# A step of a hybrid transformer on one core: two weight chunks with places of their own at the head, and a triangular inverse spread over four quarters of the matmul array

## The chip, the cores and the metric

The kernel runs as one program on one core of a Trainium2 chip. The metric is the device time of one execution in microseconds (us); lower is better. A core has five engines, each with its own queue of instructions: TensorE (PE, matmuls into PSUM), VectorE (DVE), ScalarE (ACT), GpSimd (POOL) and SyncE (SP), which here only issues DMA transfers. They wait for each other by semaphores.

## The reference

One inference step of a small backbone: two layers, width 1024, 128 context tokens and 512 latent tokens, all in float32. For each layer:

```python
h = modulate(rmsnorm(x, p['norm_mix_g']), mod[0], mod[1])       # mod = silu(c) @ w_ada + b_ada
q, k, v, u_r, u_f = split_projection(h, p['w_in'])              # 1024 -> 2176 columns
o_attn = latent_attention(axial_rope(q), axial_rope(k), v, k_ctx, v_ctx, p['attn_sink'])
o_rwkv, _, _ = rwkv_mix(u_r, s_ctx[:, 0], s_ctx[:, 1], p)       # both directions, 4 heads of 64
o_fnet = fourier_mix(u_f)
x = x + g1 * (concat(o_attn, o_rwkv, o_fnet) @ p['w_out'])      # then norm, SwiGLU (2816), residual

def step(S, inp):                                               # the scan inside rwkv_mix
    r_t, w_t, k_t, v_t, kk_t, a_t = inp
    S = (S * w_t[:, :, None, :]
         - jnp.einsum('bhvk,bhk->bhv', S, kk_t)[..., None] * (kk_t * a_t)[:, :, None, :]
         + v_t[..., None] * k_t[:, :, None, :])
    return S, jnp.einsum('bhvk,bhk->bhv', S, r_t)
```

Outputs are both token streams after a last norm, the context's keys and values, and the final scan states.

## The kernel before, in words

Channels lie on the 128 partitions and all 640 tokens on the free axis, so x is eight tiles of 128x640. A float32 weight is split on the chip: ACT copies it into a high half of the type float32r (`weight_high`), POOL subtracts to get the low half (`weight_low`), and three matmuls make one product.

**Weights and the ring.** SP loads the weights in chunks of mostly 1 MB, in the fixed order of the list CHUNKS, into a ring of four slots (`ring`). A chunk is issued only when the chunk four places earlier has been used (`ada_done` for modulation weights "ada", `wl_ready` for projection weights "rw"). For layer 0 the order begins ada 0 to 3, rw 0, ada 4 to 7, rw 1. Two ada chunks make one call of `ada_rows` (L957), 32 thin matmuls written into a PSUM bank; a copy (`row_copy`, DVE or ACT) and `ada_cols` (L966) turn them into columns of the table `mod`.

**The head of layer 0.** PE transposes x in ten halves of 128x512 (L863); ACT copies each out of PSUM. ACT squares x tile by tile into the two buffers `sq`, PE adds them over channels (`norm_part`, L872), ACT takes the root, DVE the reciprocal, PE spreads it (`inverse(0)`). Then PE does `ada_rows(0)`, `inverse(0)`, `ada_cols(0)`, some idle matmuls for warming (`warm`), `ada_rows(1)` and `ada_cols(1)`. DVE builds the first half of `mod` and the gain, scales x, ACT adds the shift, DVE makes the low half, and PE starts the first two units of the projection with `ada_rows(2)` and `ada_rows(3)` between their halves. POOL issues 15 small parameter loads first, then its memsets (`mn_zero`), for which ACT waits before its first copy.

**The recurrence.** The scan over tokens is done in chunks of 64 tokens. A pair is a 128x128 block: two chunks (`ck`) by two heads (`hd`). Four pairs make a group, and the five groups of a layer run in two calls: groups 0 and 1, then, after the rest of the attention, groups 2 to 4. Each pair p owns PSUM banks 2p and 2p+1. For a group:

1. `token_tiles`: four transposes a pair (L1273 to L1276), which ACT copies to SBUF (L1755).
2. Products of the scaled rows (L1306, L1309, L1312): twelve 64x64 or 64x128 matmuls a pair; each float32 matmul counts as two instructions.
3. DVE multiplies the product A B by the mask of the first level (L2235), the other products by the masks (L2237), and adds the unit matrix (L2242): T0.
4. The inverse of the unit triangular matrix of 64x64, by six levels of doubling. PE first puts T0 and its transpose into PSUM (L1322, L1325). Levels 1 to 5: PE multiplies B by the inverse so far (L1334), DVE masks the product (P1, L2256), PE adds P1 Y and X P1 to what stands in PSUM (L1341, L1346; in the last level L1349 makes another product), and ACT copies both, 256 columns (XY, L1767). Every step goes over the four pairs in turn; a pair's step is at `ps` rows of its own chunk, so inputs and output lie on the same half of the partitions.
5. Two more products (L1356; L1364 to L1373), then the chain over chunks, one after the other: L1392 makes the next state, L1397 the output, DVE scales and adds (L2287, L2300, L2303). In the chain of groups 0 and 3, at steps 4 and 5, PE issues two pairs' token tiles of the next group ahead.

POOL takes no part in the recurrence but for loads of states (L804), stores of final states (L825) after group 2, and half the scaling (`by_r_and_rate`, L814). The next weights after it are those of w_out (NPROJ).

Of the kernel before, what the change touches and what calls it, by code (L numbers as in the profile page):

```python
# [12 lines left out]
KT = D // 128  # L13
# [14 lines left out]
SLOTS = 4  # L28
# [38 lines left out]
CHUNKS = chunk_order()  # L67
# [206 lines left out]
def build(nc, I, O):  # L274
# [7 lines left out]
    with ctx:  # L282
# [180 lines left out]
        w_ready = [sem(f"w_ready{s}") for s in range(SLOTS)]  # L463
        wh_ready = sig("wh_ready", NUNIT)
# [47 lines left out]
        prod_ps, l0_sb, lp_sb, t0_sb = (sig(x_, n2) for x_ in ("prod_ps", "l0_sb", "lp_sb", "t0_sb"))  # L512
# [25 lines left out]
        xT_ps, xT_sb, c_ready = sem("xT_ps"), sem("xT_sb"), sem("c_ready")  # L538
# [28 lines left out]
        def unit_weights(l, u):  # L567

            _, ck, g, nk = UNITS[u]
            n = CHUNK_AT[(l,) + ck]  # L570
            raw_w = ring[:, n % SLOTS, 0:2 * nk * 128].rearrange("p (k c) -> p k c", k=nk)
# [16 lines left out]
            return n, raw_w[:, :, 128 * g:128 * g + 128], parts[0], parts[1]  # L588
# [60 lines left out]
        def _(e):  # L649
# [25 lines left out]

            for n, (l, kind, i) in enumerate(CHUNKS):
                if (kind, i) == ("rw", 2):
                    tables_of(l)
# [64 lines left out]
        def _(e):  # L743
            own = Own(e, pool_own)
            params(e, 0)

# [5 lines left out]
            nc.gpsimd.memset(csil[:, :, :], 0.0).then_inc(mn_zero, 1)  # L752
            e.wait_ge(mn_zero, 5)
            e.wait_ge(xT_ps, 11)
            for l in range(DEPTH):

                def weight_low(u):
                    n, raw_w, hi, lo = unit_weights(l, u)
                    e.wait_ge(wh_ready.sem, wh_ready.upto(l, u + 1))
                    nc.gpsimd.tensor_tensor(lo, raw_w, hi, SUB).then_inc(wl_ready(), 1)  # L760
# [87 lines left out]
        def _(e):  # L848
# [7 lines left out]
            for t in range(5):  # L856
                e.wait_ge(ld_x[t], 16)
                for g in range(2):
                    n = 2 * t + g
                    if n >= 2:  # L860
                        e.wait_ge(xT_sb, n - 1)
# [5 lines left out]
            e.wait_ge(xT_sb, 10)  # L867
# [15 lines left out]
            for l in range(DEPTH):  # L883
# [5 lines left out]
                def chunk(name, of=None):  # L889
                    n = CHUNK_AT[(l if of is None else of,) + name]  # L890
                    e.wait_ge(w_ready[n % SLOTS], READY[n])
                    return ring[:, n % SLOTS, :]
# [6 lines left out]
                def norm_part(la, which, k):  # L899

                    e.wait_ge(sq_ready.sem, sq_ready.upto(la, which * KT + k + 1))
# [136 lines left out]

                if l == 0:
                    for k in range(KT):  # L1040
                        norm_part(0, 0, k)

                e.wait_ge(ld_prow[l], 16 * 15)
                lat, cx = begin(("small", 0))
                tr(lat[:, 0:NPR], prow[:, :], ident[0:NPR, 0:NPR]).then_inc(acc_ready(), 1)
                if l == 0:
                    ada_rows(0, l)
                    inverse(0)
                    ada_cols(0, l)
                    warm(8)  # L1050
                    ada_rows(1, l)
                    ada_cols(1, l)
# [204 lines left out]
                def recurrence(first, last_group, items_before, pairs_before):  # L1257
# [4 lines left out]

                    def token_tiles(g, n):
# [14 lines left out]
                    tiled = 0  # L1278
                    for g in range(first, last_group):
# [6 lines left out]
                        if g > first and tiled < ng:  # L1286
# [10 lines left out]
                        for n in range(tiled, ng):  # L1297
                            token_tiles(g, n)
                        tiled = 0
                        for n, (p, ht, d, t) in enumerate(group):  # L1300
                            e.wait_ge(tok_sb.sem, tok_sb.upto(l, base + n + 1))
                            H, A_, R_, K_, B_ = row_of[ht]
                            tiles = [(hd, rows_of[hd], ck, rows_of[ck], slice(128 * t + 64 * ck, 128 * t + 64 * ck + 64))
                                     for ck in range(2) for hd in range(2)]
                            for hd, hs, ck, cs, c in tiles:
# [1289 lines left out]
```

## Time and profile before

| what | value |
|---|---|
| three runs | 1905.29, 1906.85 (median), 1908.67 us |
| the profiled execution | 1905.69 us, of which the span from the first to the last instruction is 1903.9 us |
| mean granted clock of TensorE | 0.994 of full speed |
| DMA | 161.25 MB, mean 85 GB/s over the span |

The profile is that of one execution. A busy engine is one with an instruction running; PE's weight loads (PEld) run beside its matmuls. An arrow in brackets names what ended the idle time before a row. Rows with the same line, one after the other, stand merged with their count.

### The profile page before, as it was taken

What the parts mean: (1) busy time and instruction counts of PE and PEld (TensorE: products, weight loads), DVE (VectorE), ACT (ScalarE), POOL (GpSimd) and SP (SyncE); (2) the same over time, 40 slices, a digit from 0 to 9 for tenths busy, and PEclk for the clock granted to TensorE, in tenths of its full rate; (3) what the DMA queues carried; (4) which work ended last, traced back from release to release, by engine and by line L of the source; (5) the groups of instructions that cost most, each with busy time, mean ns of one, the idle gap of its engine ahead of it and who ended that gap; (6) DMA issues with size and microseconds to landing.
All of it is one profiled execution on the core that took longest, in us unless ns stands there. A gap on an engine that the chain in (4) does not pass through costs nothing. (4 is left out here: it accounts for less than half of the span.)

```text
span 1903.9 us, 48376 instructions
## 1 busy us (share of the span) xinstructions
PE 1806.2 (95%) x20973; PEld 1704.9 (90%) x20973; DVE 1053.7 (55%) x2344; ACT 828.6 (44%) x1736; POOL 348.7 (18%) x230
## 2 busy tenths in 40 slices
PE   6899889999999999999999997989999999999997
PEld 5899678888989999999989986969888999999997
DVE  2433866655196483747453358474536828556563
ACT  4332655553165253434433256455424525434352
POOL 3233300011211203020233440000032030111112
PEclk8999999999999999999999999999999999999999
DMA  8753600001632423232327343000012132321311
GB/s 266 249 152 103 180 4 3 3 7 27 199 89 68 111 67 99 63 94 73 94 80 214 101 137 84 4 2 7 26 45 65 53 105 62 95 81 62 96 63 56
DMA packets 215950, 161.25 MB, mean 85 GB/s; under 512 B 21969, under 2 KB 213147, under 8 KB 215739
## 3 DMA queue, kind: packets, MB, share of 16 engines
q1 hardware_dynamic: 213818, 156.13, 27.9%
q8 instruction: 167, 2.74, 0.6%
q0 software_dynamic: 1920, 2.03, 0.3%
q14 instruction: 45, 0.36, 0.1%
HBM read 154.99 MB, written 3.15 MB: 83 GB/s over the span
## 5 line engine op out<-in xcount | busy, mean ns | idle before, releaser
L2365 DVE SCALAR_TENSOR_TENSOR x<-PS,mod,x 128x320 f32<-128x320 f32 (+2 forms) x240 | 90.7, 433 | 295.1 <-PE PS L998 295.1
L1033 PE MATMUL PS<-T_hi,wsplit 128*128 128x320 f32 x768 | 170.0, 309 | 0.0
L997 PE MATMUL PS<-in_hi,win 128*128 128x320 f32 x480 | 150.6, 321 | 1.6 <-ACT mix L1621 0.9
L760 POOL TENSOR_TENSOR SfR<-ring,SfR 128x768 fp32r<-128x768 f32 (+1 forms) x24 | 41.1, 1711 | 582.0 <-ACT SfR L1571 582.0
L998 PE MATMUL PS<-in_hi,win 128*128 128x320 f32 x480 | 144.9, 309 | 0.0
L1767 ACT ACTIVATE mix<-PS 128x256 f32<-128x256 f32 x240 | 92.5, 385 | 98.5 <-PE PS L1346 43.0
L997 PE MATMUL PS<-hid_hi,wsplit 128*128 128x320 f32 x440 | 133.1, 310 | 0.0
L998 PE MATMUL PS<-hid_hi,wsplit 128*128 128x320 f32 x440 | 132.5, 309 | 0.0
L1033 PEld LDWEIGHTS PS<-T_hi,wsplit 128*128 128x128 f32 x768 | 128.5, 188 | 0.0
L1033 PE MATMUL PS<-h_hi,wsplit 128*128 128x320 f32 x576 | 127.6, 309 | 0.0
L1033 PE MATMUL PS<-T_lo,wsplit 128*128 128x320 f32 x384 | 118.7, 309 | 0.0
L1852 ACT ACTIVATE wsplit<-Sf 128x512 fp32r<-128x512 f32 x96 | 59.8, 629 | 130.0 <-DVE Sf L2415 72.3
L2435 DVE TENSOR_TENSOR E<-E,PS 128x320 f32<-128x320 f32 x120 | 58.5, 488 | 87.5 <-PE PS L1033 87.2
L760 POOL TENSOR_TENSOR win<-ring,win 128x1024 fp32r<-128x1024 f32 x30 | 72.5, 2417 | 175.5 <-ACT win L1571 175.3
L1571 ACT ACTIVATE win<-ring 128x1024 fp32r<-128x1024 f32 x30 | 31.8, 1061 | 159.1 <-PE PS L998 136.2
L760 POOL TENSOR_TENSOR wsplit<-ring,wsplit 128x768 fp32r<-128x768 f32 (+2 forms) x42 | 74.5, 1779 | 119.5 <-ACT wsplit L1571 119.5
L1033 PEld LDWEIGHTS PS<-h_hi,wsplit 128*128 128x128 f32 x576 | 96.4, 188 | 0.0
L997 PEld LDWEIGHTS PS<-in_hi,win 128*128 128x128 f32 x480 | 90.2, 188 | 6.1 <-issue 4.7
L998 PEld LDWEIGHTS PS<-in_hi,win 128*128 128x128 f32 x480 | 90.3, 188 | 2.4 <-issue 2.4
L2256 DVE TENSOR_TENSOR mix<-PS,lvl 128x128 f32<-128x128 f32 x200 | 49.2, 291 | 75.2 <-PE PS L1334 75.0
L1033 PE MATMUL PS<-h_lo,wsplit 128*128 128x320 f32 x288 | 89.0, 309 | 0.0
L997 PEld LDWEIGHTS PS<-hid_hi,wsplit 128*128 128x128 f32 x440 | 82.6, 188 | 0.5 <-issue 0.5
(492 smaller groups left out, 5543.2 us busy)
## 6 DMA issues: line engine op xcount, KB each, us to landing
ring<-in_w_ada SPq DMA_DIRECT2D x48, 1024.0 KB, 7.4
ring<-in_ffn_w_in SPq DMA_DIRECT2D x88, 512.0 KB, 5.0
ring<-in_ffn_w_out SPq DMA_DIRECT2D x16, 768.0 KB, 4.3
ring<-in_ffn_w_out SPq DMA_DIRECT2D x16, 640.0 KB, 4.0
ring<-in_w_in SPq DMA_DIRECT2D x8, 1024.0 KB, 6.7
ring<-in_w_in SPq DMA_DIRECT2D x10, 512.0 KB, 5.8
ring<-in_w_in SPq DMA_DIRECT2D x16, 256.0 KB, 5.7
ring<-in_w_out SPq DMA_DIRECT2D x16, 256.0 KB, 6.5
```

Of the source, the lines that this page charges most:

```text
L760: nc.gpsimd.tensor_tensor(lo, raw_w, hi, SUB).then_inc(wl_ready(), 1)
L997: mm(lat[:, 0:TH], w, v[:, 0:TH], start=(n == 0), stop=(n == total - 1))
L998: last = mm(cx[:, 0:TH], w, v[:, TH:T], start=(n == 0), stop=(n == total - 1))
L1033: last = mm(bank[:, 0:TH], (w_lo if p == 1 else w_hi)[:, k, :], (v_lo if p == 2 else v_hi)[:, k, :], start=(q in (A11, A12, S1_) and k == ...
L1571: act(hi, raw_w, ACT.Copy).then_inc(wh_ready(), 1)
L1767: act(XY[p].rearrange("p a t -> p (a t)"), ps[2 * p + 1][:, 0:256], ACT.Copy).then_inc(xy_sb(), 1)
L1852: act(hi, raw_b, ACT.Copy).then_inc(bh_ready(), 1)
L2256: V.tensor_tensor(P1[p], ps[2 * p][:, 0:128].rearrange("p (a t) -> p a t", a=2), lvl[:, d, lv:lv + 1, :].to_broadcast([128, 2, 64]), MUL). ...
L2365: last = V.scalar_tensor_tensor(x[:, m, a:b], bank[:, at:at + b - a], mod[:, gate_at + m, s:s + 1], x[:, m, a:b], MUL, ADD)
L2435: V.tensor_tensor(v, v, bank[:, 0:TH], op).then_inc(ps_taken(), 1)
```

## The change

Two chunks, rw 0 and ada 4 of layer 0, leave the ring's order and get places in a buffer that is free at that time; SP issues them after the first four ring chunks, with no wait. On PE `ada_rows(0)` goes ahead of the norm sums; `ada_cols(0)` and `ada_rows(1)` go ahead of `inverse(0)`, and the warming matmuls behind `ada_cols(1)`; the parameter transpose stands amid the sums. Copies of x out of PSUM and squares of x are taken by ACT and DVE in turn; the copy of c and of the parameters goes to DVE; POOL's memsets go ahead of its loads.

In the recurrence A B is formed transposed, into the other half of the partitions, together with the other products; POOL adds the unit matrix to it in place; DVE's masks contain the unit matrix too, so that P1 is the unit matrix plus the masked product and PSUM need not accumulate. X moves to the other bank and the other half of the partitions, so that the matmuls for X and Y of one level lie on different quarters of the array and are issued in turn. The fifth level's extra product goes into its first part. In the chains of groups 0 and 3, at steps 6 and 7, the products of two pairs of the next group are issued ahead.

The lists and the loads, on SP:

```diff
-CHUNKS = chunk_order()
+SIDE = ((0, "rw", 0), (0, "ada", 4))
+CHUNKS = [c for c in chunk_order() if c not in SIDE]
...
+        side_at = [mixv(S2_AT, SLOT_W), mixv(22150, SLOT_W)]
...
             for n, (l, kind, i) in enumerate(CHUNKS):
+                if n == SLOTS:
+                    side(0)
+                    side(1)
```

On POOL; the last call stands after the stores of the final states:

```diff
+                def unit_diagonals(g):
+
+                    for n, (p, ht, d, t) in enumerate(GROUPS[g]):
+                        e.wait_ge(lp_sb.sem, lp_sb.upto(l, 4 * g + n + 1))
+                        nc.gpsimd.tensor_tensor(LP[p][:, :, BA, :], LP[p][:, :, BA, :],
+                                                eye64[:, :].unsqueeze(1).to_broadcast([128, 2, 64]), ADD).then_inc(
+                                                    diag_sb(), 1)
+
                 state_in(0)
                 by_r_and_rate(0)
+                unit_diagonals(0)
                 state_in(1)
+                for g in range(1, 4):
+                    unit_diagonals(g)
...
+                unit_diagonals(4)
```

On PE, the head:

```diff
                 if l == 0:
+                    ada_rows(0, l)
+                    e.wait_ge(xT_sb[0], 5)
+                    e.wait_ge(xT_sb[1], 5)
                     for k in range(KT):
                         norm_part(0, 0, k)
-
-                e.wait_ge(ld_prow[l], 16 * 15)
-                lat, cx = begin(("small", 0))
-                tr(lat[:, 0:NPR], prow[:, :], ident[0:NPR, 0:NPR]).then_inc(acc_ready(), 1)
-                if l == 0:
-                    ada_rows(0, l)
+                        if k == 3:
+                            small()
+                    ada_cols(0, l)
+                    ada_rows(1, l)
                     inverse(0)
-                    ada_cols(0, l)
+                    ada_cols(1, l)
                     warm(8)
-                    ada_rows(1, l)
-                    ada_cols(1, l)
```

On PE, the recurrence:

```diff
+                    halves = [(hd, ck, rows_of[ck], rows_of[1 - ck]) for hd in range(2) for ck in range(2)]
+                    def products(g, n):
...
+                        for hd, hs, cs, os, c in tiles:
+                            mm(ps[2 * p + hd][os, 128:192], H[hs, B_ + d, c], H[hs, A_ + d, c], start=True, stop=True)
+                        for hd, hs, cs, os, c in tiles:
+                            mm(ps[2 * p + hd][cs, 0:128], H[hs, K_ + d, c], H[hs, d:d + 3:2, c], start=True, stop=True)
+                        for hd, hs, cs, os, c in tiles:
+                            last = mm(ps[2 * p + hd][cs, 192:256], H[hs, B_ + d, c], H[hs, R_ + d, c],
+                                      start=True, stop=True)
...
-                        for n in range(tiled, ng):
+                        for n in range(ahead_, ng):
                             token_tiles(g, n)
...
+                        for n in range(ahead_, 2):
+                            products(g, n)
+                        ahead_ = 0
+                        products(g, 2)
+                        first_inverse(g, 0)
+                        products(g, 3)
+                        for n in range(1, ng):
+                            first_inverse(g, n)
...
-                                for hd, ck, cs in halves:
-                                    last = mm(ps[2 * p][cs, 64 * hd:64 * hd + 64], LP[p][cs, hd, BA, :],
-                                              XY[p][cs, 2 + hd, :], start=True, stop=True)
+                                for hd, ck, cs, os in halves:
+                                    if lv == 5:
+                                        mm(ps[2 * p][cs, 128 + 64 * hd:192 + 64 * hd], LP[p][cs, hd, KA, :],
+                                           TOK[p][cs, tV, 64 * hd:64 * hd + 64], start=True, stop=True)
+                                    last = mm(ps[2 * p + 1][cs, 128 + 64 * hd:192 + 64 * hd], LP[p][os, hd, BA, :],
+                                              XY[p][os, 2 + hd, :], start=True, stop=True)
...
-                                for hd, ck, cs in halves:
-                                    mm(b1[cs, 64 * hd:64 * hd + 64], P1[p][cs, hd, :], XY[p][cs, hd, :],
-                                       start=False, stop=(lv == 5), skip_group_check=True)
...
+                                for hd, ck, cs, os in halves:
                                     if lv < 5:
-                                        last = mm(b1[cs, at_x], XY[p][cs, hd, :], P1[p][cs, hd, :],
-                                                  start=False, stop=(lv == 4), skip_group_check=True)
...
+                                        mm(ps[2 * p + 1][os, 64 * hd:64 * hd + 64], XY[p][cs, hd, :], P1[p][cs, hd, :],
+                                           start=True, stop=True)
+                                    last = mm(ps[2 * p][cs, 64 * hd:64 * hd + 64], P1[p][cs, hd, :], XY[p][cs, hd, :],
+                                              start=True, stop=True)
...
+                            if g in (0, 3) and i in (6, 7):
+                                products(g + 1, i - 6)
+                                ahead_ = 2
```

On ACT:

```diff
+                        def inverse_copy(lv, n):
...
+                            src = ps[2 * p][:, 0:256] if lv == 5 else PS[:, 2 * p:2 * p + 2, 0:128]
```

On DVE:

```diff
-                            V.tensor_tensor(P1[p], PS[:, 2 * p:2 * p + 2, 256:320],
-                                            lvl[:, d, 0:1, :].to_broadcast([128, 2, 64]), MUL).then_inc(l0_sb(), 1)
...
-                            V.tensor_tensor(T0[p], P1[p], eye64[:, :].unsqueeze(1).to_broadcast([128, 2, 64]),
-                                            ADD).then_inc(t0_sb(), 1)
+                        def first_level(n):
+                            p, ht, d, t = group[n]
+                            e.wait_ge(diag_sb.sem, diag_sb.upto(l, base + n + 1))
+                            V.tensor_tensor(T0[p], LP[p][:, :, BA, :], lvl[:, d, 0:1, :].to_broadcast([128, 2, 64]),
+                                            MUL).then_inc(t0_sb(), 1)
+
+                        factors(0)
+                        for n in range(1, ng):
+                            factors(n)
+                            first_level(n - 1)
+                        first_level(ng - 1)
```

And in the table of the levels' masks:

```diff
+        lv[:, :, n] += (i == t)[:, None, :]
```

## Rows read from the trace of the kernel before

**Rows 1.** The page's first and second part: busy time; granted clock by slice.

```profile
PE 1806.2 (95%) x20973; PEld 1704.9 (90%) x20973; DVE 1053.7 (55%) x2344; ACT 828.6 (44%) x1736; POOL 348.7 (18%) x230
PEclk8999999999999999999999999999999999999999
```

**Rows 2.** Busy time by stretch: stretch, length, each engine, then PEclk, DMA share, GB/s.

```profile
255.60:317.50 61.90, 57.19 (x1818) 54.51 (x1818) 34.93 (x119) 26.50 (x67) 2.48 (x4) 1.00 0.02 5
15.00:20.00 5.00, 3.30 (x20) 2.42 (x18) 0.00 (x0) 4.02 (x8) 0.00 (x0) 1.00 1.10 348
25.00:30.00 5.00, 5.00 (x81) 3.49 (x81) 1.15 (x1) 2.56 (x5) 0.00 (x0) 0.50 0.00 0
69.60:255.60 186.00, 175.52 (x1589) 158.18 (x1589) 97.64 (x161) 83.02 (x189) 61.97 (x33) 1.00 0.48 140
```

**Rows 3.** Timeline, two levels of the first group: start, length, then engine and line.

```profile
264.22 0.89 DVE L2256 TENSOR_TENSOR mix<-PS,lvl 128x128 f32<-128x128 f32 x4
264.56 0.45 PE L1341 MATMUL PS<-mix 64*64 64x64 f32 x8
266.48 1.10 PE L1334 MATMUL PS<-mix 64*64 64x64 f32 x32
267.41 0.40 PE L1341 MATMUL PS<-mix 64*64 64x64 f32 x8
268.09 1.79 ACT L1767 ACTIVATE mix<-PS 128x256 f32<-128x256 f32 x4 [1.01 <-PE PS L1346]
269.28 1.10 PE L1334 MATMUL PS<-mix 64*64 64x64 f32 x32
```

**Rows 4.** Timeline of PE, products of the second group.

```profile
290.04 0.29 PE L1306 MATMUL PS<-h 64*64 64x64 f32 x8
290.15 0.40 PE L1309 MATMUL PS<-h 64*64 64x128 f32 x8
```

**Rows 5.** ACT copies: timeline of four of 512 columns, then groups by form.

```profile
256.58 2.07 ACT L1755 ACTIVATE mix<-PS 128x512 f32<-128x512 f32 x4
...
L1755 ACT ACTIVATE mix<-PS 128x512 f32<-128x512 f32 x40 | 21.5, 599 | 27.2 <-PE PS L1276 27.0
L1767 ACT ACTIVATE mix<-PS 128x256 f32<-128x256 f32 x240 | 92.5, 385 | 98.5 <-PE PS L1346 43.0 <-PE PS L1325 33.4 <-PE PS L1349 10.2
```

**Rows 6.** Timeline between products and levels, second group; then DVE by form.

```profile
289.44 0.34 PE L1306 MATMUL PS<-h 64*64 64x64 f32 x8
292.49 0.68 DVE L2237 TENSOR_TENSOR mix<-PS,masks 128x512 f32<-128x512 f32 x1
293.49 0.68 DVE L2237 TENSOR_TENSOR mix<-PS,masks 128x512 f32<-128x512 f32 x1
295.00 1.13 PE L1334 MATMUL PS<-mix 64*64 64x64 f32 x32
...
L2242 DVE TENSOR_TENSOR mix<-mix,eye 128x128 f32<-128x128 f32 x40 | 11.3, 281 | 0.0
```

**Rows 7.** POOL additions by form; then timeline of POOL beside DVE.

```profile
L830 POOL TENSOR_TENSOR mix<-mix 128x640 f32<-128x640 f32 x12 | 18.9, 1574 | 16.9 <-ACT mix L1520 16.9
L760 POOL TENSOR_TENSOR wsplit<-ring,wsplit 128x768 fp32r<-128x768 f32 x20 | 36.9, 1854 | 59.0 <-ACT wsplit L1571 59.0
...
69.59 2.69 POOL L760 TENSOR_TENSOR win<-ring,win 128x1024 fp32r<-128x1024 f32 x1
69.94 2.49 DVE L2045 SCALAR_TENSOR_TENSOR mix<-mix,par 128x128 f32<-128x128 f32 x1
```

**Rows 8.** Timeline of PE at the head.

```profile
24.94 1.39 PE L872 MATMUL PS<-mix,mats 128*32 128x160 f32 x16 [0.23 <-ACT mix L1520]
26.64 3.64 PE L957 MATMUL PS<-ring,csil 128*32 128x128 f32 x64
35.42 1.96 PE L957 MATMUL PS<-ring,csil 128*32 128x128 f32 x64
52.33 1.95 PE L957 MATMUL PS<-ring,csil 128*32 128x128 f32 x64 [2.95 <-DMA ring<-in_w_ada]
```

More of the change, by code:

```diff
@@ L463, in build, with chunk_at, landed @@
         w_ready = [sem(f"w_ready{s}") for s in range(SLOTS)]
+        side_ready = [sem(f"side_ready{s}") for s in range(len(SIDE))]
+        side_at = [mixv(S2_AT, SLOT_W), mixv(22150, SLOT_W)]
+        def chunk_at(key):
+            return side_at[SIDE.index(key)] if key in SIDE else ring[:, CHUNK_AT[key] % SLOTS, :]
+        def landed(e, key):
+            if key in SIDE:
+                e.wait_ge(side_ready[SIDE.index(key)], 16)
+            else:
+                e.wait_ge(w_ready[CHUNK_AT[key] % SLOTS], READY[CHUNK_AT[key]])
         wh_ready = sig("wh_ready", NUNIT)
@@ L1538, in norm_shift @@
                     last.then_inc(h_ready(), 1)
-            e.wait_ge(xT_sb, 10)
+            for q_ in range(2):
+                e.wait_ge(xT_sb[q_], 5)
             for l in range(DEPTH):
@@ L1549, in _ @@
                 if l == 0:
-                    for k in range(KT):
-                        norm_square(0, 0, k)
+                    for k in range(0, KT, 2):
+                        if k >= 2:
+                            e.wait_ge(sq_used.sem, sq_used.upto(0, k - 1))
+                        act(sq[:, 0, :], x[:, k, :], ACT.Square).then_inc(sq_first[0], 1)
                 norm_root(l, 0)
-                free, lat, cx = ready(("small", 0))
-                act(par[:, :], lat[:, 0:NPR], ACT.Copy).then_inc(free(), 1)
-                taken(e, l, ("small", 0))
-                act(omka[:, :], par[:, PR_KA:PR_KA + 2], ACT.Copy, scale=-1.0, bias=1.0).then_inc(par_ready(), 1)
+                if l > 0:
+                    free, lat, cx = ready(("small", 0))
+                    act(par[:, :], lat[:, 0:NPR], ACT.Copy).then_inc(free(), 1)
+                    taken(e, l, ("small", 0))
+                    act(omka[:, :], par[:, PR_KA:PR_KA + 2], ACT.Copy, scale=-1.0, bias=1.0).then_inc(par_ready(), 1)
                 def weight_high(u, of=None):
@@ L1764, in recurrence @@
                         for lv in range(6):
-                            for n, (p, ht, d, t) in enumerate(group):
-                                e.wait_ge(xy_ps.sem, xy_ps.upto(l, 6 * base + lv * ng + n + 1))
-                                act(XY[p].rearrange("p a t -> p (a t)"), ps[2 * p + 1][:, 0:256],
-                                    ACT.Copy).then_inc(xy_sb(), 1)
+                            for n in range(ng):
+                                inverse_copy(lv, n)
                         for n, (p, ht, d, t) in enumerate(group):
@@ L2019, in _ @@
                 if l == 0:
+                    row_copy(0)
+                    free, lat, cx = ready(("small", 0))
+                    V.tensor_copy(par[:, :], lat[:, 0:NPR]).then_inc(free(), 1)
+                    taken(e, l, ("small", 0))
+                    V.tensor_scalar(omka[:, :], par[:, PR_KA:PR_KA + 2], -1.0, 1.0, MUL, ADD).then_inc(par_ready(), 1)
                     norm_inverse(l, 0)
-                    row_copy(0)
                     row_copy(1)
```

151 lines of the change are left out of this document (81 added, 70 removed).

## The prediction

> **What bounds the kernel now.** I read four views: the page, the busy time by stretch, the timeline of the engines, and the groups by line and form. The page's first part shows TensorE (PE) busy for 95% of the span, VectorE (DVE) for 55%, ScalarE (ACT) for 44%; its second part shows a granted clock below nine tenths in the first slice alone [rows 1]. So most of the time is PE's, and only what shortens PE's own work, or a wait of PE, is worth anything.
>
> By stretch, two places are different from the dense matmuls. The recurrence runs in four stretches, two per layer, ten groups in all; in the first of them PE is busy for 57.2 of 61.9 us, with the clock at 1.00 [rows 2], and the others look the same. These are small 64x64 matmuls, so the question is how fast PE takes them. And at the head, from 25 to 30 us, the DMA engines move nothing (0 GB/s, after 348 GB/s from 15 to 20 us), while PE works at half clock, 0.50, which is 1.2 instead of 2.4 GHz [rows 2]: the ring's four slots are full of modulation weights that nobody has used yet.
>
> **The levels of the inverse.** In the timeline one level of a group of four pairs is: 32 matmul instructions at L1334, then 64 at L1341 and L1346, then the next level. It begins at 266.48 us and the next at 269.28: 2.80 us, of which the first part takes 267.41 - 266.48 = 0.93 and the second 269.28 - 267.41 = 1.87 [rows 3]. That is 29 ns for each instruction in both, and PE has no gap: a level is PE's. All these matmuls lie on two of the four 64x64 quarters of the array (rows 0-63 to columns 0-63, rows 64-127 to columns 64-127).
>
> The change gives the second part four quarters: X goes to the crossed quarters and Y to the straight ones, taken in turn. The first part moves to the crossed quarters, but there are still only two, so it stays at 0.93. What a matmul on four quarters costs is in the trace already: the products of L1306 use all four, and eight instructions of 64 columns take 290.15 - 290.04 = 0.11 us, 14 ns each [rows 4]. So the second part falls to 64 x 14.5 ns = 0.93, and PE's work in a level from 2.80 to 1.86. In the fifth level the matmul that was last in the second part goes to the first, onto free quarters, at nothing; the saving is the same.
>
> The Trainium skill speaks against this: its page "TensorE: Matmul & The Clock Gate", section "Wait — 56ns, not 53.3ns?", says that the start of one matmul follows the start of the one before by 25 ns at least, however narrow they are. By that the second part would take 64 x 25 ns = 1.6 us and a level about 2.6 (an estimate from that page); the 14 ns above do not agree with it.
>
> Is PE then still what bounds a level? PE takes instructions in order, so the second part of pair 0 stands behind the first part of pair 3, which waits for ACT's copy of pair 3 of the level before. The loop: from the start of the second part to ACT's first copy now 268.09 - 267.41 = 0.68, of which 0.47 is PE's own time for that pair [rows 3]; with 0.23 it is 0.45 to 0.50, I take 0.50. Then three more copies: ACT's mean for this copy is 385 ns and its neighbours overlap; four copies of 512 columns at 599 ns take 2.07 us, a spacing of 0.49, 0.11 less than their duration [rows 5]. So 256 columns are spaced by about 0.275: 0.83 for three. The last copy takes 0.385 and I allow 0.10 to reach PE (from DVE's first product at 264.22, some 0.28 long by its like in rows 6, to PE at 264.56 it is 0.06 [rows 3]). Then the first part of pair 3, 0.23. Sum 0.50 + 0.83 + 0.485 + 0.23 = 2.05 us. DVE is not in it: its product of pair 0 has long ended. Low end: PE alone, 1.86. High end: copies that don't overlap, 0.45 apart, 2.57. I take 2.05, because the overlap is in the rows. Saved: 0.75 a level, 5 levels x 10 groups = 50 levels: **37.5 us** (11 to 47).
>
> **Before the levels.** From the first product to the first level a group takes 295.00 - 289.44 = 5.56 us; DVE sets it with three operations a pair, and the pairs follow each other by 1.00 us (292.49 to 293.49) [rows 6]; two of the three are of 128x128, the third of 128x512. The change drops one of the small ones, about 0.2 of the 1.00 as it overlaps its neighbour, and puts an addition on GpSimd (POOL) between the two others, so the pairs come at 0.8 but each has POOL in its chain. No row shows an addition of 128x128 on POOL: 640 columns take 1.57 us and 768 take 1.85, so 128 by that slope about 0.45; ends 0.28 (DVE's own time for such a one [rows 6]) and 1.57. I take 0.5 plus 0.2 to start; it lies beside the next pair's DVE work, and shows once, behind the last pair. In POOL's queue ahead of it are only loads of states and work for the first head pair that is finished before the group begins; behind it stand the stores of the states and the low halves of w_out, needed after the recurrence. DVE has an operation of another task between this stage and the first level in every group, so that the earlier end is partly given back there. I count 0.2 us for a group whose products all still come after the token tiles (6 groups). In the other 4 groups two pairs' products are issued in the chain of the group before, where PE waits for DVE; that brings them, and DVE's first factors, forward by about 1 us. PE's next chain step behind such a product comes 0.44 later. Together **5 us**, with ends of 0 and 12 by POOL's ends.
>
> POOL and DVE can also block each other. At 69.94 us a DVE operation of 128x128 with two SBUF inputs took 2.49 us beside a POOL operation that ran from 69.59 for 2.69 [rows 7], where a product of that size and kind of inputs takes 0.28 [rows 6]: it waited till POOL was done. The Trainium skill, "SBUF — State Buffer", section "Who interferes with whom", has the rule: a DVE operation with two SBUF inputs and a POOL operation that reads SBUF exclude each other, and the first to start holds the port. In this case the T0 product has two SBUF inputs and meets POOL's addition for the next pair; but it starts first, as its engine needs no wake-up, and the factors beside it read PSUM. If POOL is first each time, it is 0.4 us for each pair, 1.6 per group, 16 us in all. I take it at 0.
>
> **The head.** Now: the norm's sums, a pair of them 1.39 us, paced by squares on ACT alone; then the first row products at 26.64, 3.64 us at half clock; only then is a slot free, and the fourth row products start at 52.33, after a wait of 2.95 us for their weights [rows 8]. After: the two side chunks follow the four ring chunks without a wait; at 348 GB/s [rows 2] a chunk of 1 MB takes 3.0 us. The four are in by 24, so the side chunks by 30 and ada chunks 5 to 7 by 39, if their slots come free in time; they do, if the first and second rows end before about 33. The first rows need two chunks (about 18 us); at half clock they end near 21.8. Then four pairs of norm sums at about 1.7 (the squares of a pair now run together, but each waits for its buffer): 28.5. The second rows at half clock, 3.6: 32. From their end to the point where PE is ready for the fourth rows it is now 52.33 - 2.95 - (35.42 + 1.96) = 12.0 us [rows 8], work that the change leaves as it is: 44. The weights come at 39.5, or 42.8 if POOL's mask tables, 1.2 MB, are carried in between. So 44 for 52.33, and I call it **8.5 us** with the copies of x. At full clock PE would be there at 39 and the weights decide: at most 13; with the norm sums late by two more pairs, 5. From 69.6 to 255.6 us PE is busy for 175.5 of 186 [rows 2] and the view of waits names no DMA there, so the gain is kept. Moving the copies of x, the parameter columns and POOL's memsets costs nothing that is late: the first rows wait for weights until 18 us.
>
> **Sum.** 37.5 + 5 + 8.5 = 51 us, off the profiled execution's 1905.7 (its span is 1903.9): 1854.7. That execution is 1.2 us under the median of the three runs. Forecast: 1855.
>
> **Rivals.**
> 1. ACT bounds the levels: copies from two banks don't overlap, 2.57 us a level. For it: ACT already needs 0.385 a copy and PE leaves less room. Against: the 0.49 spacing [rows 5]. Saves 11.5 + 13.5: 1881.
> 2. The four quarters don't overlap in this order, since X and Y of a pair come from the same rows back to back, while the products of L1306 alternate rows. Then a level stays at 2.80 and 13.5 is left: 1892. Against: the 14 ns [rows 4]. By the floor of the Trainium skill's page "TensorE: Matmul & The Clock Gate", named above, a level of 2.6 would give 1882, an estimate that no row bears out.
> 3. POOL's addition costs 1.57, near the row for 640 columns, and holds DVE: the stage before the levels takes some 2.5 us longer in each group, 25 less 5 and the rest as forecast: 1885.
> 4. Slower: the granted clock falls in the levels. PE will have gaps of about 0.2 us in each level where it had none, and at the head the clock fell to 0.50 after a stretch with PE busy 3.30 of 5 us [rows 2]. A level at half clock is 2 x 1.86 plus some 0.2 of latency, 3.9 us instead of 2.05; the gain of 51 is gone when 28 of 50 levels run so. With all: 1905.7 + 50 x 1.1 - 8.5 = 1952. Against: PE would still be busy for nine tenths of a level, and in the recurrence, whose chains make it wait as it is, the clock stands at 1.00 [rows 2].
>
> **How the numbers follow.** Forecast or near it 0.72; rival 1 0.10; rival 2 0.07; rival 3 0.05; rival 4 or another loss of that size 0.06. The forecast's own range, from the ends above taken two thirds of the way, is 1838 to 1872; with all low ends at once it is 1834. To leave out no more than 0.2 it reaches to rivals 1 to 3: 1836 to 1892. No change means within 0.2%, 3.8 us, about what a measurement of this kernel can tell: only a mix of rivals ends there. Faster 0.91, same 0.03, slower 0.06.
>
> **What would show it.** In the timeline the second part of a level with 16 instructions a pair in 0.23 us (rival 2: 0.47), the levels 2.05 apart, and PE's waits at the first part released by ACT; ACT's four copies 0.28 apart (rival 1: 0.45). POOL's additions near 0.5 us and DVE's T0 at 0.28, without long ones. At the head no stretch without DMA before 39 us, the second rows done by 32, the fourth begun near 44. The clock at 1.00 in the four stretches. The forecast is wrong if the levels don't come closer than 2.5 us.

## The result, and the profile after

The changed kernel takes 1893.27 us, the median of five runs (1883.86 to 1896.24); the kernel before took 1906.85 beside it. The ratio is 0.992, with a 95% interval of 0.9896 to 0.9944: about 14 us faster where 51 were forecast. The profiled execution took 1893.27 us, its span is 1891.5.

First the page of the changed kernel: busy time, granted clock by slice, and the queue that carries instructions (packets, MB, share).

```profile
PE 1766.6 (93%) x20973; PEld 1661.0 (88%) x20973; DVE 1063.6 (56%) x2316; ACT 805.5 (43%) x1723; POOL 364.1 (19%) x270
PEclk9999999999999999999999999999999999999999
...
q8 instruction: 166, 2.72, 0.6%
```

PE is busy for 40 us less than in [rows 1], with the same number of matmuls, but the span is only 12 us shorter: work went, waits came. Busy time by stretch of the changed kernel (the columns are those of [rows 2]): the first recurrence stretch, the head from 25 us, the levels of the first group, and its chain.

```profile
248.19:309.05 60.86, 50.34 (x1818) 46.61 (x1816) 34.42 (x110) 23.21 (x66) 5.31 (x12) 0.93 0.02 5
...
25.00:30.00 5.00, 4.53 (x98) 3.42 (x99) 2.82 (x6) 4.18 (x5) 0.58 (x1) 1.00 1.10 349
255.26:268.37 13.11, 10.54 (x494) 10.11 (x488) 6.62 (x22) 5.85 (x20) 1.42 (x3) 1.00 0.03 9
...
274.00:282.00 8.00, 7.03 (x113) 5.86 (x116) 3.41 (x15) 1.19 (x2) 0.00 (x0) 0.64 0.01 2
```

The stretch of [rows 2] was 61.9 us with PE busy for 57.2; it is 60.9 with PE busy for 50.3. The clock is 1.00 in the levels, but 0.64 in the chain behind them. From 25 to 30 us DMA moves 349 GB/s where it moved nothing. The head did what was forecast (PE's timeline, second and fourth row products):

```profile
27.07 1.95 PE L994 MATMUL PS<-ring,csil 128*32 128x128 f32 x64
...
43.38 1.84 PE L994 MATMUL PS<-ring,csil 128*32 128x128 f32 x60 [0.90 <-DMA ring<-in_w_ada]
```

The fourth begin 8.95 us sooner than in [rows 8], and the recurrence 7.7 us sooner (248.19 for 255.89, first token tile). What is missing is in the recurrence. ACT's copies in the levels of the first group, one row per level unless a level is broken up:

```profile
257.29 1.21 ACT L1815 ACTIVATE mix<-PS 128x256 f32<-128x256 f32 x4 [1.34 <-PE PS L1398]
259.32 1.21 ACT L1815 ACTIVATE mix<-PS 128x256 f32<-128x256 f32 x4 [0.82 <-PE PS L1398]
261.36 0.94 ACT L1815 ACTIVATE mix<-PS 128x256 f32<-128x256 f32 x3 [0.82 <-PE PS L1398]
263.33 0.39 ACT L1815 ACTIVATE mix<-PS 128x256 f32<-128x256 f32 x1 [1.03 <-PE PS L1398]
264.53 1.21 ACT L1815 ACTIVATE mix<-PS 128x256 f32<-128x256 f32 x4 [0.82 <-PE PS L1398]
267.94 1.21 ACT L1815 ACTIVATE mix<-PS 128x256 f32<-128x256 f32 x4 [2.19 <-PE PS L1398]
```

The first three levels are 2.03 and 2.04 us apart, the forecast's 2.05 for the 2.80 of [rows 3]; four copies take 1.21, so they are 0.275 apart, and PE's first part of the next level starts a pair 0.06 us behind each copy's end. Then the third level is torn: its last copy comes 1 us late, the next level 3.17 us after, the one behind that 3.41. PE's timeline has a gap at both places, and the view of waits, summed over the first two groups from 255 us (line and what it waited for, us in total, times, longest), has the same name for most of PE's idle time:

```profile
262.96 0.21 PE L1396 MATMUL PS<-mix 64*64 64x64 f32 x1 [0.99 <-issue]
...
266.96 0.21 PE L1387 MATMUL PS<-mix 64*64 64x64 f32 x1 [1.27 <-issue]
```

```profile
PE PS L1387 <- issue: 2.1, 2, 1.3
PE PS L1441 <- DVE St L2371: 1.6, 2, 0.8
PE PS L1396 <- issue: 1.3, 2, 1.0
PE PS L1417 <- issue: 1.1, 1, 1.1
PE PS L1422 <- issue: 1.1, 1, 1.1
```

"issue" is idle time in which the engine waited for nothing that the profile shows. So I numbered TensorE's instructions in the trace in order (weight loads, matmuls, event waits), and set beside the gaps the 16 KB packets of the instruction queue. A gap here runs from the start of the last instruction before it to the start of the next; the idle time alone, as the views above count it, is some 0.2 us shorter (0.99 for 1.21).

```
gap of PE          us    number of the     number    packet of q8 that
                         instruction       mod 256   came before it
261.75..262.96     1.21       5313           193     260.53..261.46
265.48..266.96     1.49       5569           193     264.61..265.53
272.87..274.15     1.28       6081           193     271.84..272.80
293.64..294.21     0.57       7105           193     291.86..292.79
296.65..297.66     1.01       7361           193     295.30..296.25
303.55..304.84     1.29       7873           193     302.25..303.59
```

Every one stands at the same place modulo 256. In the two layers' recurrence there are 28 gaps over 0.5 us with that remainder, 32.1 us in all, of which 23.1 in the levels; the kernel before has 4, 2.5 us. The program has 42,654 TensorE instructions and 166 packets, one for 257; it has as many per level as before (192, which are 96 matmuls and their 96 weight loads, and the waits). In the levels of the second group, split in 40 slices of 0.296 us, four packets are seen:

```profile
GB/s 0 0 55 0 0 0 0 0 0 0 0 0 0 0 55 0 0 0 0 0 0 0 0 0 0 0 55 0 0 0 0 0 0 0 0 0 0 55 0 0
...
q8 instruction: 4, 0.07, 1.9%
```

They start at 288.31, 291.86, 295.30 and 298.80: 3.44 to 3.55 apart. Under load the shortest distances in the whole trace are 3.35 to 3.5. A level of 2.03 us with 192 instructions would use up 256 in 2.7 us; at 2.80 it was 3.7.

The stages of a group, summed over the ten groups (us; from the first token tile to the first product of level 1, levels to the product behind level 5, that product, the chain's products until the chain's first output, the chain from there, less the overlap with the next group):

```
              tiles   levels   behind   to chain   chain   overlap    sum
before         82.9    142.5     15.4      33.3     35.7     -4.0    305.7
after          82.0    126.0     16.3      37.5     42.3     -6.8    297.3
```

### The profile page after: what moved, and what is told of

Its sections match the earlier page's. It is cut to its first block and busy times, and to the rows that moved or that the text cites. A ratio compares the mean times of both kernels' runs of the same rounds, so it can differ in the third digit from the quotient of the medians.

```text
span 1891.5 us, 48336 instructions
## 1 busy us (share of the span) xinstructions
PE 1766.6 (93%) x20973; PEld 1661.0 (88%) x20973; DVE 1063.6 (56%) x2316; ACT 805.5 (43%) x1723; POOL 364.1 (19%) x270
## 3 DMA queue, kind: packets, MB, share of 16 engines
q0 software_dynamic: 1920, 2.03, 0.3%
## 5 line engine op out<-in xcount | busy, mean ns | idle before, releaser
L1815 ACT ACTIVATE mix<-PS 128x256 f32<-128x256 f32 x240 | 77.2, 388 | 93.5 <-PE PS L1398 65.1
L1621 ACT ACTIVATE win<-ring 128x1024 fp32r<-128x1024 f32 x30 | 31.9, 1062 | 160.1 <-PE PS L1035 135.9
L843 POOL TENSOR_TENSOR mix<-mix,eye 128x128 f32<-128x128 f32 x40 | 16.4, 410 | 371.1 <-DVE mix L2312 371.1
L2340 DVE TENSOR_TENSOR mix<-PS,lvl 128x128 f32<-128x128 f32 x200 | 53.0, 291 | 57.5 <-PE PS L1389 57.0
```

Of the source, the lines that this page charges most:

```text
L1621: act(hi, raw_w, ACT.Copy).then_inc(wh_ready(), 1)
L1815: act(dst, src, ACT.Copy).then_inc(xy_sb(), 1)
L2340: V.tensor_tensor(P1[p], ps[2 * p + 1][:, 128:256].rearrange("p (a t) -> p a t", a=2), lvl[:, d, lv:lv + 1, :].to_broadcast([128, 2, 64]), ...
```

## The experiments

The 256 instructions of one 16 KB packet are called a page of instructions here. Theory S: in the levels TensorE's instructions do not come fast enough, one page of 256 in no less than about 3.45 us. Rival C: the granted clock, 0.988 for 0.994 in the spans, eats the gain. Rival A: the array's quarters, or the copies that pace them, don't hold 2.03 us. The code cuts of this section are shortened: the arguments `start`, `stop` and `skip_group_check` are left out, and those of e2 and e5 are outlines of the code.

**e1, half the instructions, the same columns** (the second head's weights are left out).

```diff
-mm(ps[2*p+1][cs, 128+64*hd:192+64*hd], LP[p][os, hd, BA, :], XY[p][os, 2+hd, :])
+if hd == 0: mm(ps[2*p+1][cs, 128:256], LP[p][os, 0, BA, :], XY[p][os, 2:4, :])
...  (X and Y likewise)
```

> The changed kernel with half as many TensorE instructions in the five levels: each product of a level takes the weights of the first head alone and moves 128 columns through them where two heads had 64 each; the second head's weights are left out, so the output is not the reference's. Columns through the array, copies, masks and waits stay. Theory S (supply): TensorE's instructions arrive in pages of 256, one page in no less than about 3.45 us, and the changed levels use one up in 2.7; the gaps of 0.5 to 1.8 us inside the levels vanish, the time from the first product of level 1 to the product behind level 5 falls from a mean of 12.6 us to 10.2-10.8 in each of the 10 groups, and the program goes from 1893 to about 1870 (1864 to 1878). Theory C (clock): the gain was eaten by the lower granted clock (0.988 against 0.994); levels stay at 12.6 and the time at 1888-1897. Theory A (array): four quarters with 64 columns cannot hold 2.03 us per level for long; columns are the same, so 12.6 and 1893 again.

Measured: 1857.54 us (1856.43 to 1862.02), ratio to before 0.9747 (0.9734 to 0.9761). The levels come to 105.1 us in the ten groups, 10.5 each, the recurrence to 265.6; one gap over 0.5 us is left at the page ends. ACT's copies in the first group, all five levels:

```profile
256.51 1.21 ACT L1818 ACTIVATE mix<-PS 128x256 f32<-128x256 f32 x4 [1.33 <-PE PS L1401]
258.51 1.21 ACT L1818 ACTIVATE mix<-PS 128x256 f32<-128x256 f32 x4 [0.79 <-PE PS L1401]
260.52 1.21 ACT L1818 ACTIVATE mix<-PS 128x256 f32<-128x256 f32 x4 [0.79 <-PE PS L1401]
262.52 1.21 ACT L1818 ACTIVATE mix<-PS 128x256 f32<-128x256 f32 x4 [0.79 <-PE PS L1401]
264.51 1.21 ACT L1818 ACTIVATE mix<-PS 128x256 f32<-128x256 f32 x4 [0.77 <-PE PS L1401]
```

2.00 us apart without a break. S holds in the levels, which come to what it expected. The time is lower than it expected (36 us under the changed kernel instead of 23), as the other stages gain too: those behind the levels, the four last columns above, go from 89.3 to 81.3, the tiles from 82.0 to 79.3. A and C fall as main causes: the changed kernel's clock is 1.00 in all its levels, while in e1 10.1 us of the levels, in the fifth, sixth and tenth group, ran at half clock, and yet they are shorter.

**e7, the other direction: a third more instructions, 4% more columns.**

```diff
+mm(ps[2*p+1][cs, 128+64*hd:136+64*hd], LP[p][os, hd, BA, :], XY[p][os, 2+hd, 0:8])
 mm(ps[2*p+1][cs, 128+64*hd:192+64*hd], LP[p][os, hd, BA, :], XY[p][os, 2+hd, :])
```

> The changed kernel with each first product of a level done twice, the extra time with 8 columns (written over at once): 64 instructions a level more, 256 in place of 192, with 4 per cent more columns. Theory S: a level costs one page, 3.45 us, against a mean of 2.5 now: levels of a group 16.5-17.3 us instead of 12.6, the program 1930-1942. Theory A and C: the extra work fits beside the copies that pace that product (0.28 us a tile against 0.13); within 5 us of 1893.

Measured: 1940.76 us (1934.3 to 1943.9), ratio 1.0178 (1.016 to 1.0195). The levels sum to 180.6 us, 18.1 a group, a little over what S expected. ACT's copies, levels 1 to 5 of the first group:

```profile
258.71 1.21 ACT L1817 ACTIVATE mix<-PS 128x256 f32<-128x256 f32 x4 [1.77 <-PE PS L1400]
261.60 1.21 ACT L1817 ACTIVATE mix<-PS 128x256 f32<-128x256 f32 x4 [1.68 <-PE PS L1400]
264.85 1.21 ACT L1817 ACTIVATE mix<-PS 128x256 f32<-128x256 f32 x4 [2.04 <-PE PS L1400]
268.30 1.21 ACT L1817 ACTIVATE mix<-PS 128x256 f32<-128x256 f32 x4 [2.24 <-PE PS L1400]
271.92 1.21 ACT L1817 ACTIVATE mix<-PS 128x256 f32<-128x256 f32 x4 [2.40 <-PE PS L1400]
```

The time is what S expected, but the run does not tell S from a plainer cause that neither expectation priced: the doubled product takes PE twice as long. The first two rows are 2.89 us apart, and PE has no stop between them: in its timeline the first part of that level, 32 matmuls of 8 columns and 32 of 64, runs from 259.15 to 260.98 us, 29 ns a matmul, as with 64 columns alone. So the level is 0.86 longer than the 2.03 of the changed kernel; over 50 levels that is 43 of the 55 us by which the levels grew. The stops at page ends in the levels come to 24.7 us, counted from 0.1 us up, for 24.1 in the changed kernel: hardly more. What bears on S is that the next three distances, with one stop in each, are 3.25, 3.45 and 3.62 us, over the 2.89 that PE needs.

**e8, the edit of e1 in the kernel before.**

```diff
-mm(ps[2*p][cs, 64*hd:64*hd+64], LP[p][cs, hd, BA, :], XY[p][cs, 2+hd, :])
+if hd == 0: mm(ps[2*p][cs, 0:128], LP[p][cs, 0, BA, :], XY[p][cs, 2:4, :])
...  (X and Y likewise)
```

> The kernel before with the edit of e1 in its levels: half the TensorE instructions, each with 128 columns through the first head's weights, the second head's weights left out (not the reference's output). Theory S: in the kernel before a page of 256 instructions lasts 3.7 us in the levels, longer than the 3.45 in which one arrives, so supply takes little there: levels stay within 0.6 us of 14.25 a group (two quarters and the columns through them are the same) and the program within 1898-1908. Rival A2: what e1 gained came from the halved weight loads, not from the supply; then the same edit gives the same 20 us of levels here, 1870-1888.

Measured: 1899.05 us (1897.97 to 1899.8), ratio 0.9957 (0.9941 to 0.9974). Levels 13.5 us a group for 14.25, a little more than the 0.6 allowed; the copies of the first levels are 2.67 apart for 2.80:

```profile
265.31 1.70 ACT L1770 ACTIVATE mix<-PS 128x256 f32<-128x256 f32 x4 [1.23 <-PE PS L1349]
267.98 1.70 ACT L1770 ACTIVATE mix<-PS 128x256 f32<-128x256 f32 x4 [0.97 <-PE PS L1349]
270.65 1.70 ACT L1770 ACTIVATE mix<-PS 128x256 f32<-128x256 f32 x4 [0.97 <-PE PS L1349]
```

The edit is worth 7 us here and 36 in the changed kernel. The halved weight loads by themselves are the small part (A2 falls; in the changed kernel, too, they take a level without a stop only from 2.03 to 2.00): the kernel before was just below the limit of the supply, the changed one is beyond it.

**e3 and e4, the two parts of the change alone** (the hunks of the head, and those of the recurrence, on the kernel before).

> The kernel before with the head part of the change alone. Theory S: recurrence as before (levels 14.2 us a group), time 7.7 us lower as the stages in the changed kernel's trace add up: 1899 (1896 to 1902). Theory C: the head part also sets the pattern of the clock behind it, so the granted clock falls to about 0.988 here too and most of the 7.7 us is given back: 1904-1908.

> The kernel before with the recurrence part of the change alone. Theory S: the five levels take 12.6 us a group against 14.2, but 11 us come back behind them; gaps at every 256th instruction; 1901 (1897 to 1905). Theory C: with the old head the clock stays at 0.994 and the predicted 42 us of the recurrence come out: 1865-1880.

Measured: the head alone 1897.33 us (1894.64 to 1900.67), ratio 0.9952 (0.9939 to 0.9964), clock 0.994 in the profiled run; the recurrence alone 1898.6 (1894.33 to 1900.94), ratio 0.9955 (0.9941 to 0.9968), clock 0.987, levels 127.9 us, 30 gaps at page ends. The two sum to 0.9907, within the interval of the whole. S foresaw both. C as it was put fails on both: the head does not bring the lower clock, and without the new head the recurrence part gains no more than with it. That the recurrence part lowers the clock itself (0.987 with the old head) is not excluded by these two runs. PE's longest waits in the first two groups of e4 have the name that they have in the whole change:

```profile
PE PS L1356 <- issue: 1.8, 2, 1.0
PE PS L1365 <- issue: 1.7, 2, 1.0
```

**e6, TensorE kept busier in the chains.**

```diff
+for o in rows_of:
+    mm(ps[2*p+hf][o, 320:512], Qt[p][o, hf, :], TOK[p][o, 0:3, 0:64])
 for o in rows_of:
     last = mm(ps[2*p+hf][o, 192:256], St[ht][o, d, slot, :], Qt[p][o, hf, :])
```

> The changed kernel with one product of 192 columns more per half and step of the chains, into columns that nobody reads, to keep TensorE busier there (64 instructions a group more). Theory C (the lower clock behind the recurrence groups eats the gain): the granted clock rises from 0.988 to 0.993 or more and 6 to 10 us come back: 1883-1888. Theory S: the stalls at page ends stay, the clock is a by-product; no gain, 1890 to 1900.

Measured: 1903.04 us (1899.79 to 1908.47), ratio 0.9984 (0.9973 to 0.9995), clock 0.991. The filler's columns lie in banks whose sums are still open, and the run is read for TensorE's work alone, not for its outputs. In the first group's chain the clock stays up, for the 0.64 above:

```profile
274.00:282.00 8.00, 7.51 (x156) 6.72 (x156) 4.10 (x16) 1.20 (x2) 0.00 (x0) 1.00 0.02 4
```

The levels stay at 126.6 us and 27 gaps at page ends; the chains go from 42.3 to 51.1 with the filler in them. So the stops at page ends stay with the clock up in that chain, as S says. More on the clock this run cannot tell: 11.8 us of its levels, in the fifth, sixth and tenth group, ran at half clock, and the filler costs more than it can give.

**e2, fewer instructions by a full-array product** (both chunks of the level's first product in one 128x128 weight tile with zeros in two blocks, laid out by GpSimd; half of the first inverse also takes both heads in one product, which the cut does not show).

```diff
-for hd, ck: mm(ps[2*p+1][cs, 128+64*hd:192+64*hd], LP[p][os, hd, BA, :], XY[p][os, 2+hd, :])
+for hd:     mm(ps[2*p+1][:,  128+64*hd:192+64*hd], LX[p][:, hd, :, :],   XY[p][:, 2+hd, :])
```

> The changed kernel, same result, with fewer TensorE instructions: the first product of a level takes both chunks in one 128x128 weight load with zeros in the two unused blocks (GpSimd lays that tile out once per tile and group, two products of some 0.4 us each), so 32 instead of 64 instructions for it per level; one half of the first inverse takes both heads in one product. A level has 160 instead of 192 instructions. Theory S: a page lasts 3.25 us in the levels against 3.45 to fetch one, so levels run at 2.05-2.2 us where they now average some 2.55, the stage of five levels falls from 12.6 to 10.6-11.2 us, and the program goes from 1893 to about 1877 (1868 to 1885), under both kernels. Theories C and A: the full-array load takes no column away; no change within 3 us, or slower by the added GpSimd work (1893-1900).

Measured: 2045.55 us, the median of four runs (2029.94 to 2052.1), ratio 1.0722 (1.068 to 1.0765); two more took 2064.86 and 2071.92. A miss for every theory. Busy time in the levels of the first group, around those of the second, and in the stage before the levels of the third; then DVE's masks:

```profile
255.90:287.00 31.10, 31.10 (x403) 28.35 (x398) 8.17 (x22) 7.18 (x19) 3.88 (x6) 0.51 0.01 4
304.00:325.00 21.00, 20.21 (x416) 18.31 (x418) 9.01 (x23) 6.55 (x21) 2.60 (x4) 0.92 0.01 3
371.00:378.00 7.00, 5.14 (x148) 4.50 (x148) 3.51 (x8) 3.21 (x7) 3.46 (x9) 1.00 0.01 4
```

```profile
262.83 0.29 DVE L2359 TENSOR_TENSOR mix<-PS,lvl 128x128 f32<-128x128 f32 x1 [0.56 <-PE PS L1407]
263.68 0.29 DVE L2359 TENSOR_TENSOR mix<-PS,lvl 128x128 f32<-128x128 f32 x1 [0.56 <-PE PS L1407]
```

The full-array product takes 0.85 us a tile at a clock of 0.51, where ACT's copies pace the quarter products at 0.275. In the levels of seven groups, 28.9 to 31.9 us long, the clock is at its lower level (1.2 of 2.4 GHz) for most of the time. In those of the second, fifth and tenth group, 18.7 to 19.8 us long, it is at the upper one for most: there the masks of one level are 0.45 us apart (309.09, 309.54, 309.98, 310.43) and the levels 3.02. PE is busy almost throughout in both kinds (31.10 of 31.10 us in the first group, 19.15 of 19.15 in the fifth), so a PE busy without a gap is not enough to explain the lower clock, and its cause is not shown. My estimate for that product was wrong at either level; on S this run says nothing.

**e5, a level of one round trip, and a third fewer instructions.** The product Q = L'X, formed anew at each level, can be carried along: X becomes XP and Q becomes QP, with P the masked Q (' is the transpose). With P as weights, Y = X' and Q' stand side by side as one moving block of 128 columns.

```diff
-P = mask * (L'X)              # product 1, DVE mask
-X = Y'P;  Y = P'Y             # products 2 and 3, ACT copy
+P = mask * Q                  # DVE
+Q = (Q')'P;  [Y, Q'] = P'[Y, Q']   # two products, ACT copy
```

Two tiles are issued in turn, one on straight, the other on crossed quarters. P has two buffers, so that DVE can write the next while the second product runs.

> The changed kernel, same result, with a level of two products instead of three: the first product of a level, Q = L'X, is no longer formed anew but carried along with X (Q goes to Q P, X to X P), so a level is one pass through the array, one mask and one copy, and 128 instead of 192 TensorE instructions; two tiles are worked together, one of them changing its partition half at each level, so that all four quarters still work side by side; half of the mask products is merged as in the kernel before. A group has 992 instead of 1280 TensorE instructions up to the end of the levels. Theory S (pages of 256 instructions in no less than 3.45 us each): a level takes about 1.73 us (128/256 x 3.45), the stage from the first Q to the product behind level 5 about 10 us where the levels of the changed kernel take 12.6, and the program comes to 1850-1880, best 1866, below the changed kernel. Theory A (the array or the copies bound the levels): columns through the array stay the same and copies stay at four of 0.28 us a level, so no gain over 1893 beyond 5 us.

Measured: 1862.74 us (1858.99 to 1865.25), ratio to before 0.9771 (0.9757 to 0.9785): 44 us under the kernel before, and below every run of the changed one. ACT's copies, two a pair of tiles, and the page's instruction queue:

```profile
259.86 0.66 ACT L1840 ACTIVATE mix<-PS 128x256 f32<-128x256 f32 x2 [0.32 <-PE PS L1377]
260.69 0.66 ACT L1840 ACTIVATE mix<-PS 128x256 f32<-128x256 f32 x2 [0.17 <-PE PS L1377]
261.51 0.66 ACT L1840 ACTIVATE mix<-PS 128x256 f32<-128x256 f32 x2 [0.17 <-PE PS L1377]
...
q8 instruction: 155, 2.54, 0.6%
```

A pair of tiles takes 0.83 us, a level 1.65, and at 128 instructions a level a page lasts 3.3 us. The levels sum to 96.5 us (9.65 a group) and the recurrence to 266.5; 16 gaps at page ends remain in the program, 17.7 us, and 37.9 us still go to the products ahead of the chains. This is the version that beats both kernels. A falls, which gave it 5 us at most; as the edit also takes a third of PE's instructions out of a level, the run alone does not tell supply from PE's own work.

## Why the prediction was wrong

The step that failed is the sum of the levels: "2.05", saved "0.75 a level", 5 levels x 10 groups. The working behind the 2.05 was right and is in the rows: 2.03 us a level, copies 0.275 apart, PE released by ACT. But the 50 levels take 126.0 us, 2.52 each. The step counted what the array, ACT and DVE need and left out that 192 instructions must also reach TensorE. The row that would have given it away was on the page of before, third part (packets, MB, share):

```profile
q8 instruction: 167, 2.74, 0.6%
```

The packets have 16 KB each and, in the trace of before, came mostly 3.3 to 4.6 us apart in the levels and behind them, when a level took 2.80.

- Levels: 37.5 us forecast, 16.5 measured (142.5 to 126.0). The 21.0 us missing stand beside 23.1 us of stops at page ends in the levels. In e1, where the supply is enough, 37.4 are saved (to 105.1).
- Stage before the levels: 5 forecast, 0.9 measured; e1 has 79.3, so 3.6. One part is the collision of POOL and DVE, taken at 0: two of the 40 T0 products took 2.41 us, 4.3 us over the others in all. POOL's addition and DVE's T0 by form, then one of the two long ones:

```profile
L843 POOL TENSOR_TENSOR mix<-mix,eye 128x128 f32<-128x128 f32 x40 | 16.4, 410 | 371.1 <-DVE mix L2312 371.1
...
L2320 DVE TENSOR_TENSOR mix<-mix,lvl 128x128 f32<-128x128 f32 x40 | 15.7, 393 | 3.2 <-POOL mix L843 3.2
```

```profile
411.62 2.34 POOL L782 TENSOR_TENSOR in_lo<-ring,row_lo 128x1024 fp32r<-128x1024 f32 x1
...
411.70 2.41 DVE L2320 TENSOR_TENSOR mix<-mix,lvl 128x128 f32<-128x128 f32 x1 [0.32 <-POOL mix L843]
```

  The addition is 0.41, near the 0.5 taken, and T0's median is 0.284. But T0 took 2.41 us in the row shown, where POOL had begun its next operation on a weight 0.08 us sooner: not with the next pair's addition, as feared, but with the operation queued behind the last one. The rule in the Trainium skill, "SBUF — State Buffer", section "Who interferes with whom", fits it.
- Behind the levels nothing was forecast; 8.9 us were lost there (sum of the four last columns of the stage table, 80.4 before, 89.3 after). Page gaps stand there, and chains at half clock; e1, with one gap of 0.7 us and no half clock behind its levels, has 81.3. What each of the two takes is not shown.
- Head: 8.5 forecast, 7.7 by the stages. Its marks came true: no stretch without DMA before 39 us, the second rows done by 29.0, the fourth begun at 43.38 for 44. The way there was partly another: the second rows ran at full clock, 1.95 us instead of 3.6, and the fourth waited 0.90 us for their weights, where the forecast let PE's own work decide. That 44 was met so closely is in part luck.
- Rivals 1 to 3 are refuted (copies 0.275 apart; levels at 2.03; POOL's addition 0.41). Rival 4 had the right engine and the wrong place: the clock is 1.00 in the levels and falls in chains behind them. Its price was not isolated: of the five runs of the changed kernel the one with a clock of 0.993 took 1883.86 us, those with 0.986 1893.46 and 1896.24, so some 10 us may be the clock's; e1 at 0.993 took 1856.43, so 27 remain at the same clock. That is a reading of single runs, not shown by an experiment.
- Two sums of the prediction do not come out. Two thirds of the way to the ends of its three terms is 1841 to 1878, not 1838 to 1872; the measured 1893 lies outside both. And 64 x 25 ns with the 0.93 of the first part is a level of 2.53, not 2.6. Neither changes the forecast.

The Trainium skill, "Runtime: NRT & Kernel Launch", section "Instruction fetch mechanics", states that instructions are refilled in blocks of 16 KiB, 256 of them, and that crossing a block's end is "mostly hidden". The first half agrees with the packets here; the second holds for the kernel before (2.5 us in its recurrences) and not for the changed one (32.1).

Open: why a page takes 3.45 us when its packet is on the DMA engine for 0.93 to 1.4 only. In the table of gaps PE goes on 1.25 to 1.5 us after a packet's end, and in the levels the next packet starts 1.1 to 1.7 us after that; what fills these times is not known.

## What to carry to other kernels

Before you make small matmuls faster, take the instructions in the stage, weight loads included, divide them by 256 and multiply by the distance of instruction packets where they come closest in your trace (about 3.45 us here). For a level of the changed kernel that is 192 / 256 x 3.45 = 2.59 us; it averaged 2.52. If the product is more than the time you forecast, take it for the forecast; the gain then lies in fewer instructions with more columns each. A run with more instructions does not test this unless you know what PE takes for them without a stop, as e7 shows. "issue" as the releaser of a busy engine's waits is a question: number the instructions, and see whether the gaps come at a fixed count.

## What was not expected of the hardware

TensorE took 64x64 float32 matmuls on four quarters at 14 ns each (16 in 0.23 us), which with their weight loads is an instruction every 7 ns; but in the long run it was given one per 13.5 ns (256 in 3.45 us), and the page's end was paid as a stop of 0.6 to 1.8 us, not as a lower rate. On two quarters a matmul took 29 ns on average when half of them had 8 columns (e7), as when all had 64. And a 128x128 float32 weight tile with 64 columns cost 0.45 us for four passes at full clock; in seven of ten groups it ran mostly at half clock, in e2's first group at 0.51, where quarter tiles in the same place ran at 1.00.
